# Two transformer blocks on one core: norms cut into a latent and a context half, modulation chunks and rotary tables moved, and a first stage fed chunk by chunk from one queue

## The reference

```python
# first block; for each layer i, for latents and (while needed) context, m = silu(c) @ w_mod[i] + b_mod[i] in 9 parts
def ffn_sublayer(h, shift, scale, gate, w_in, w_out, g, b):
    y = swiglu(h * (1.0 + scale) + shift, w_in, w_out)
    return layer_norm(ALPHA * h + 0.5 * gate * y, g, b)
...
h_lat = ffn_sublayer(h_lat, m_lat[0], m_lat[1], m_lat[2], ...)         # and h_ctx
u_lat, u_ctx = modulate(h_lat, m_lat[3], m_lat[4]), modulate(h_ctx, ...)
y_lat, y_ctx = attention(u_lat, u_ctx, w_qkv, w_o, ...)                # layer 0 neighbourhood, layer 1 windowed
h_lat = layer_norm(ALPHA * h_lat + m_lat[5] * y_lat, g, b)             # and h_ctx in layer 0
h_lat = ffn_sublayer(h_lat, m_lat[6], m_lat[7], m_lat[8], ...)         # and h_ctx in layer 0
```

## Time and profile before

| | |
|---|---|
| median of 3 runs | 2751.87 us (2750.27 to 2756.49) |
| profiled execution | 2755.03 us, span 2753.0 us, mean TensorE clock 0.977 |
| busy: PE / PEld / DVE / ACT / POOL | 2626.1 / 2266.3 / 1631.3 / 1099.2 / 358.3 us |
| moved | 394.24 MB, mean 143 GB/s |

### The profile page before, as it was taken

One profiled execution on the slowest core, in us unless ns is written; L12 is line 12 of the kernel. 1 busy time (PEld: TensorE's weight loads), 2 busy tenths in 40 slices (PEclk: granted clock), 3 DMA queues, 4 the chain that ended last, 5 costly groups with the idle time before them and its releaser, 6 DMA issues.

```text
span 2753.0 us, 41075 instructions
## 1 busy us (share of the span) xinstructions
PE 2626.1 (95%) x16124; PEld 2266.3 (82%) x16124; DVE 1631.3 (59%) x2363; ACT 1099.2 (40%) x1542; POOL 358.3 (13%) x426
## 2 busy tenths in 40 slices
PE   6999998999899998999998989989899999999999
PEld 3888886877688886888887689989899899998989
DVE  4665746566574474575655755565565566565555
ACT  3221223265422223321224653444455445455453
POOL 3000023122300003200013020010001100000210
PEclk8999999999999999999999999999899999999999
DMA  6453524411253352353432035535324454432544
GB/s 241 171 183 124 195 105 141 161 64 46 96 192 132 108 187 80 137 191 138 168 130 101 32 128 186 198 143 191 117 93 153 161 199 168 168 125 77 184 168 146
DMA packets 64252, 394.24 MB, mean 143 GB/s; under 512 B 7440, under 2 KB 8944, under 8 KB 29040
## 3 DMA queue, kind: packets, MB, share of 16 engines
q1 hardware_dynamic: 41072, 308.78, 31.6%
q0 software_dynamic: 21344, 77.41, 8.1%
q10 hardware_dynamic: 1696, 6.08, 0.6%
HBM read 391.19 MB, written 1.05 MB: 142 GB/s over the span
## 4 chain that ended last, share of the span: by engine, by line
PE 84%; DVE 7%; ACT 4%; issue 2%; DMA 1%; POOL 1%; ACTq 0%; POOLq 0%; DVEq 0%
PE banks L412 24%; PE banks L414 24%; PE banks L413 24%; DVE wlo L377 3%; ACT whi L369 3%; PE banks L437 1%; PE banks L1055 1%; PE banks L439 1%; PE banks L438 1%; PE banks L1079 1%; PE banks L1066 1%; DMA shift_start<-in_w_mod 1%; PE banks L427 1%; PE banks L428 1%; PE banks L429 1%
## 5 line engine op out<-in xcount | busy, mean ns | idle before, releaser
L377 DVE TENSOR_TENSOR wlo<-raw,whi 128x2048 fp32r<-128x2048 f32 (+1 forms) x272 | 668.1, 2456 | 449.8 <-ACT whi L369 449.7
L369 ACT CAST whi<-raw 128x2048 fp32r<-128x2048 f32 (+1 forms) x272 | 548.6, 2017 | 278.1 <-PE banks L414 238.6
L412 PE MATMUL banks<-uhi,whi 128*128 128x512 f32 (+1 forms) x1648 | 601.6, 365 | 2.7 <-DVE wlo L377 2.7
L414 PE MATMUL banks<-uhi,wlo 128*128 128x512 f32 (+1 forms) x1648 | 599.8, 364 | 0.0
L413 PE MATMUL banks<-ulo,whi 128*128 128x512 f32 (+1 forms) x1648 | 599.8, 364 | 0.0
L412 PE MATMUL banks<-u2hi,whi 128*128 128x256 f32 x1312 | 375.8, 286 | 4.0 <-DVE wlo L377 3.9
L413 PE MATMUL banks<-u2lo,whi 128*128 128x256 f32 x1312 | 371.9, 283 | 0.0
L414 PE MATMUL banks<-u2hi,wlo 128*128 128x256 f32 x1312 | 371.9, 283 | 0.0
L412 PEld LDWEIGHTS banks<-uhi,whi 128*128 128x128 f32 x1648 | 309.5, 188 | 59.6 <-DVE wlo L377 3.3
L413 PEld LDWEIGHTS banks<-ulo,whi 128*128 128x128 f32 x1648 | 309.5, 188 | 55.3
L414 PEld LDWEIGHTS banks<-uhi,wlo 128*128 128x128 f32 x1648 | 309.4, 188 | 55.1
(11 more groups left out here) (382 smaller groups left out, 3904.5 us busy)
## 6 DMA issues: line engine op xcount, KB each, us to landing
raw<-in_ffn_in SPq DMA_DIRECT2D x132, 1024.0 KB, 4.8
raw<-in_ffn_out SPq DMA_DIRECT2D x48, 1408.0 KB, 6.3
mod_slot<-in_w_mod POOLq DMA_DIRECT2D x128, 512.0 KB, 3.5
raw<-in_w_merge SPq DMA_DIRECT2D x32, 1024.0 KB, 4.7
raw<-in_w_in SPq DMA_DIRECT2D x26, 1024.0 KB, 4.8
raw<-in_na_qkv SPq DMA_DIRECT2D x12, 1024.0 KB, 4.8
raw<-in_w_out SPq DMA_DIRECT2D x8, 1024.0 KB, 4.7
raw<-in_wa_qkv SPq DMA_DIRECT2D x6, 1024.0 KB, 4.8
```

The lines of the kernel that those rows point to most:

```text
L369: act.copy(whi[u % 2][:, 0:unit_size[u]], raw[u % 2][:, 0:unit_size[u]]).then_inc(hi_done, 1)
L377: dve.tensor_tensor(wlo[u % 2][:, 0:n], raw[u % 2][:, 0:n], whi[u % 2][:, 0:n].bitcast(F32), ALU.subtract).then_inc(lo_done, 1)
L412: pe.matmul(out, w_hi, x_hi[:, k, 0:T], start=(n == 0), stop=False)
L414: mm = pe.matmul(out, w_lo, x_hi[:, k, 0:T], start=False, stop=(n == len(chunks) - 1))
```

## The change

The four norms are cut into a latent part 0 and a context part 1 (`PARTS`). The last two out units run their latent halves first, then their context halves; means, variance, centring, scaling, `uhi`, `full_u` and `ulo` are made for 256 tokens at a time. POOL now makes `full_u` for both parts. The weights of the next phase's first unit are split in two pieces inside the norm. The next phase starts with its first unit on latents, then its second on latents, then the first and the second on context; for L1.q only the first unit is special, and the context norm is spread over the q units. Modulation chunks are dealt out anew: three per unit in L0.ffn0.out0, none in the first two units of L0.q. The rotary tables are made during M0.ffn0.out0, in other buffers. At the start, SP issues every load in the order of use, with `h` in four pieces; the scale part is laid out so that one chunk gives 128 features, PE makes one column of scales per chunk, and units 0 and 1 take chunk after chunk, unit 1 four chunks behind. The window tables are loaded before the norm of s=4 instead of behind it.

The helpers not shown do on one part what the functions before did on all tokens: `add_part_dve` adds a product to `h`, `part_var_dve`, `part_centre_dve`, `part_scale_dve`, `part_low_dve` are the variance, the subtraction of the mean, the multiplication by `rstd` and `ulo`; `part_square_act`, `part_rstd_act`, `part_hi_act` square, make `rstd` and `uhi`; `part_sums_pool` and `part_full_pool` add up and make `full_u`; `part_means_pe` is four 256-column float32 matmuls; `part_unit` is one half unit on one part; `split_hi_piece` and `split_lo_piece` split half of a unit's weights. Line numbers of the rows are those of the kernel before.

```diff
+    def part_product(pe, u, half, k, x_hi, x_lo, part, start, stop):
+        a, b = PARTS[part]
+        out = banks[:, bank(u, half), a:b]
+        w_hi, w_lo = cols(whi, u, k, half * P, half * P + P), cols(wlo, u, k, half * P, half * P + P)
+        pe.matmul(out, w_hi, x_hi[:, k, a:b], start=start, stop=False)
+        pe.matmul(out, w_hi, x_lo[:, k, a:b], start=False, stop=False)
+        return pe.matmul(out, w_lo, x_hi[:, k, a:b], start=False, stop=stop)
...
+    def out_in_parts_pe(pe, ph, chunks, x_hi, x_lo, s):
+        u2, u3 = ph.u0 + 2, ph.u0 + 3
+        for u in (u2, u3):
+            start_unit(pe, u)
+            for half in range(2):
+                part_unit(pe, u, half, chunks, x_hi, x_lo, 0).then_inc(latent_product, 1)
+        for cc in range(4, KC):
+            pe.wait_ge(*DVE_.at("h part", s, cc, 0))
+            part_unit(pe, u2 + (cc - 4) // 2, cc % 2, chunks, x_hi, x_lo, 1).then_inc(product, 1)
+            if cc == 4:
+                part_means_pe(pe, s, 0)
...
+    def first_latents_pe(pe, u, s):
+        pe.wait_ge(*DVE_.at("first half lo", u))
+        pe.wait_ge(evicted, u - 1)
+        for k in range(KC):
+            if k == KC // 2:
+                pe.wait_ge(lo_done, u + 1)
+            pe.wait_ge(*DVE_.at("u", s, k, 0))
+            for half in range(2):
+                mm = part_product(pe, u, half, k, uhi, ulo, 0, k == 0, k == KC - 1)
+                if s == 4 and k == KC - 1:
+                    mm.then_inc(product, 1)
+            if k == 3:
+                part_means_pe(pe, s, 1)
+    def first_two_units_pe(pe, ph, s):
+        u0, u1 = ph.u0, ph.u0 + 1
+        first_latents_pe(pe, u0, s)
+        start_unit(pe, u1)
+        for half in range(2):
+            part_unit(pe, u1, half, KC, uhi, ulo, 0)
+        for k in range(KC):
+            pe.wait_ge(*DVE_.at("u", s, k, 1))
+            for half in range(2):
+                mm = part_product(pe, u0, half, k, uhi, ulo, 1, k == 0, k == KC - 1)
+                if k == KC - 1:
+                    mm.then_inc(product, 1)
+        for half in range(2):
+            part_unit(pe, u1, half, KC, uhi, ulo, 1).then_inc(product, 1)
...
-    MOD_FIRST = {"L0.ffn0.in0": 16, "L0.ffn0.out0": 32, "L0.ffn0.in1": 40, "L0.q": 56, "L0.k": 64, "L0.ffn1.in0": 72,
+    MOD_FIRST = {"L0.ffn0.in0": 16, "L0.ffn0.out0": 32, "L0.ffn0.in1": 44, "L0.q": 60, "L0.k": 64, "L0.ffn1.in0": 72,
                  "L0.ffn1.in1": 88, "L1.ffn0.in0": 104, "L1.ffn0.out0": 120, "L1.ffn0.in1": 128}
+    MODS_PER_UNIT = {"L0.ffn0.out0": 3, "L0.k": 2, "L1.ffn0.out0": 2}
 
...
+    def start_loads(sp):
+        def chunk(n):
+            i = n % START_SLOTS
+            if n >= START_SLOTS:
+                sp.wait_ge(*PE_.at("scale column", n - START_SLOTS))
+            sp.dma_start(scale_start[:, i], A["w_mod_scale"][n]).then_inc(scale_landed[i], 16)
+            if n >= START_SLOTS:
+                sp.wait_ge(mod_done, 2 * (n - START_SLOTS + 1))
+            sp.dma_start(shift_start[:, i], A["w_mod"][n]).then_inc(shift_landed[i], 16)
+        def residual(i):
+            sp.dma_start(h[:, 2 * i:2 * i + 2], A["x"][:, 2 * i:2 * i + 2]).then_inc(x_loaded[i], 16)
+        sp.dma_start(crow[:], A["crow"]).then_inc(crow_loaded, 16)
+        sp.dma_start(v1[:], A["vec1"]).then_inc(v1_loaded, 16)
+        chunk(0)
+        load(sp, phases["L0.ffn0.in0"], 0, 0, None)
+        residual(0)
+        chunk(1)
+        chunk(2)
+        residual(1)
+        chunk(3)
+        load(sp, phases["L0.ffn0.in0"], 1, 1, None)
+        chunk(4)
+        residual(2)
+        chunk(5)
+        residual(3)
+        chunk(6)
+        chunk(7)
...
+    def scale_column_pe(pe, n):
+        pe.wait_ge(scale_landed[n % START_SLOTS], 16 * (n // START_SLOTS + 1))
+        if n >= 4:
+            pe.wait_ge(*DVE_.at("start vectors", n - 4))
+        for k in range(KC):
+            mm = pe.matmul(banks[:, 4 + n % 4, 0:2], scale_start[:, n % START_SLOTS, k * P:(k + 1) * P],
+                           c_cols[:, k, :], start=(k == 0), stop=(k == KC - 1))
+        mm.then_inc(*PE_.up(("scale column", n)))
...
+        for n in range(SCALES_AHEAD):
+            scale_column_pe(pe, n)
+        start_unit(pe, 0)
+        for k in range(KC + SECOND_BEHIND):
+            if k + SCALES_AHEAD < KC:
+                scale_column_pe(pe, k + SCALES_AHEAD)
+            if k < KC:
+                pe.wait_ge(*DVE_.at("u", 0, k))
+                chunk(0, k)
+            if k == SECOND_BEHIND:
+                start_unit(pe, 1)
+            if k >= SECOND_BEHIND:
+                chunk(1, k - SECOND_BEHIND)
...
+    def start_vectors_dve(dve, n):
+        at = VEC1["b_mod"][0] + n
+        dve.wait_ge(mod_done, 2 * (n + 1))
+        dve.tensor_scalar(vS0[:, 0, n, :], mods[:, 0, n, :], v1[:, at:at + 1], None, ALU.add).then_inc(*DVE_.up())
+        dve.wait_ge(*PE_.at("scale column", n))
+        dve.tensor_scalar(vS1[:, 0, n, :], banks[:, 4 + n % 4, 0:2], v1[:, at + KC:at + KC + 1], 1.0, ALU.add, ALU.add)\
+            .then_inc(*DVE_.up(("start vectors", n)))
+    def start_dve(dve):
         dve.wait_ge(*ACT_.at("c silu"))
         for n in range(KC):
             mod_products(dve, n, None, shift_start[:, n % START_SLOTS],
                          (shift_landed[n % START_SLOTS], 16 * (n // START_SLOTS + 1)))
-            if n == KC - 2:
+            if n == 0:
+                dve.wait_ge(v1_loaded, 16)
+            start_vectors_dve(dve, n)
+            if n == 0:
                 split_lo(dve, 0)
+                low_dve(dve, 0, T2, 0, uhi, ulo)
+            if n >= 2:
+                low_dve(dve, 0, T2, n - 1, uhi, ulo)
+            if n == 4:
+                split_lo(dve, 1, early=True)
+        low_dve(dve, 0, T2, KC - 1, uhi, ulo)
...
+    def norm_in_parts_dve(dve, s, gated_by, ready):
+        u0 = out_of(s).u0
+        split_lo(dve, u0 + 3)
+        for cc in range(4, KC):
+            add_part_dve(dve, s, cc, 0, gated_by, ready)
+        add_part_dve(dve, s, 4, 1, gated_by, ready)
+        part_var_dve(dve, s, 0)
+        for cc in range(4):
+            part_centre_dve(dve, s, cc, 0)
+        if s == 2:
+            add_part_dve(dve, s, 5, 1, gated_by, ready)
+        else:
+            for cc in range(4, KC):
+                part_centre_dve(dve, s, cc, 0)
+        dve.wait_ge(*ACT_.at("rstd", s, 0))
+        for cc in range(3):
+            part_scale_dve(dve, s, cc, 0)
+        part_low_dve(dve, s, 0, 0)
+        if s != 2:
+            add_part_dve(dve, s, 5, 1, gated_by, ready)
+        part_low_dve(dve, s, 1, 0)
+        split_lo_piece(dve, u0 + 4, 0)
+        for cc in range(3, KC):
+            if s == 2 and cc >= 4:
+                part_centre_dve(dve, s, cc, 0)
+            part_scale_dve(dve, s, cc, 0)
+            part_low_dve(dve, s, cc - 1, 0)
+            if cc == 3:
+                split_lo_piece(dve, u0 + 4, 1)
+                add_part_dve(dve, s, 6, 1, gated_by, ready)
+            if cc == LAST_ADD_AFTER:
+                add_part_dve(dve, s, 7, 1, gated_by, ready)
+        part_low_dve(dve, s, KC - 1, 0)
+        split_lo(dve, u0 + 5, early=True)
+        if s < 4:
+            context_norm_dve(dve, s, range(KC))
+    def context_norm_dve(dve, s, ccs):
+        if ccs[0] == 0:
+            part_var_dve(dve, s, 1)
+            for cc in range(4):
+                part_centre_dve(dve, s, cc, 1)
+            dve.wait_ge(*ACT_.at("rstd", s, 1))
+        for cc in ccs:
+            part_scale_dve(dve, s, cc, 1)
+            if cc < 4:
+                part_centre_dve(dve, s, cc + 4, 1)
+            if cc > ccs[0]:
+                part_low_dve(dve, s, cc - 1, 1)
+        part_low_dve(dve, s, ccs[-1], 1)
...
+    def norm_in_parts_act(act, s):
+        u0 = out_of(s).u0
...
+        for cc in (4, 5, 6):
+            part_square_act(act, s, cc, 0)
+        act.preload_act_table_set("natural_log_exp_and_others")
+        part_square_act(act, s, 7, 0)
+        part_square_act(act, s, 4, 1)
+        part_rstd_act(act, s, 0)
+        for cc in range(2):
+            part_hi_act(act, s, cc, 0)
+        split_hi_piece(act, u0 + 4, 0)
+        part_square_act(act, s, 5, 1)
+        part_hi_act(act, s, 2, 0)
+        split_hi_piece(act, u0 + 4, 1)
+        for cc in range(3, KC):
+            part_hi_act(act, s, cc, 0)
+            if cc == 3:
+                part_square_act(act, s, 6, 1)
+            if cc == LAST_ADD_AFTER:
+                part_square_act(act, s, 7, 1)
+        split_hi(act, u0 + 5, early=True)
+        if s < 4:
+            context_norm_act(act, s, range(KC))
...
+    def norm_in_parts_pool(pool, s):
+        for cc in range(4):
+            part_sums_pool(pool, s, cc, None)
+        for cc in (4, 5, 6):
+            part_sums_pool(pool, s, cc, 0)
+        part_sums_pool(pool, s, 4, 1)
+        for cc in range(KC):
+            part_full_pool(pool, s, cc, 0)
+            if cc == 1:
+                part_sums_pool(pool, s, 5, 1)
+            if cc == 3:
```

(82 more changed lines are left out.)

364 lines of the change are left out of this document (231 added, 133 removed).

## The result

The changed kernel took 2710.59 us (median of four, 2707.16 to 2715.45) beside 2754.18 us for the kernel before on the same chip: ratio 0.9844, 95% interval 0.9823 to 0.9866. The prediction was 2702.5 us with a range of 2687 to 2719. The time is 8.1 us above it. Of these, 2.3 come from the kernel before, whose median is 2754.18 us here and was 2751.87 when the prediction was written: 49.4 us of gain were forecast and 43.6 measured. The terms that fell short are two, the norms and the start. The profiled execution took 2708.93 us, 46.1 less than that of before.

The account below looks back on a forecast made before the run. TensorE, busy 95% of the span, was taken as the bound, leaving only idle and low-clock time to gain. Norms 29.6, start 14.8, modulation 1.4 and tables 3.6 summed to 49.4 us: 2705.6 profiled, 2702.5 median, range 2687 to 2719.

Parts of the forecast that it names:

- slower by the clock: Rival: short waits hold TensorE at 1.2 GHz behind norms and at the start, 50 us slower than now; chance 0.03.
- does nothing: Rival: the chain moves to weights, splits late by a whole norm each time, 2752 us; chance 0.02.
- Hardly a stall: Rival: norms 41, start 18.4, modulation 2.8, tables 4.2, 66 us gained in all, 2686 us; chance 0.1.
- The norms, 29.6 predicted: Four norms hidden under half products: 7.7 each at s=1 and s=3, 5.3 at s=2, 8.9 at s=4; bounds 19, 43.5.
- I take between the ends, near the average row: 1.8 us lost: Norms: stalls from GpSimd's full_u, between none at half a microsecond each and about 4.5 us per norm at 1.25.
- 24.1 to 26.9: Behind an FFN's norm: when u1's split weights are ready, in us after the last out product's latent half; wanted at 24.4.
- s=2, 5.3 predicted: Norm behind L0.wo: cover only 12.9 us; 9.8 less 4.5 for late u1 and u3 weights and GpSimd.
- Rival 1: GpSimd and VectorE shut each other out in every norm; norms give 19, all 39 us, 2713 us; chance 0.2.
- The start, 14.8 predicted: Start through unit 1: its end moves from 71.84 to 57 us, 14.8 gained; bounds 11.8 and 18.4.
- I take 57, nearer the first: Start: unit 1's end, between 53.4 if TensorE kept up and 60 at the upper end of the scale columns' cost.
- Modulation, 1.4 predicted: L0.q's 2.66 us wait goes (2.8 with restart), 1.4 lost at L0.ffn0.out0's end; net 1.4, bounds 0 and 2.8.
- Tables, 3.6 predicted: The 4.20 us wait before M0.z's third unit goes, last squares delayed 0.6; 3.6 gained, bounds 2 and 4.2.

Follow-up runs that it names:

- norms_old: The changed kernel with all four norms back in the old order, new start, modulation chunks and tables kept: 2734.49 us, ratio 0.9929 to the kernel before.
- no_full: The changed kernel without GpSimd's full_u in the norms; VectorE forms ulo from h, shift left out: 2703.39 us, ratio 0.9819 to the kernel before.
- full_unused: The changed kernel with ulo formed from h without the shift, GpSimd still making every full_u, unread by the subtraction: 2705.47 us, ratio 0.9832 to before.
- one_scale: The changed kernel with one of the eight matmuls of each scale column at the start, output not the reference's: 2707.64 us, ratio 0.983 to before.
- best_ahead3: Three start scale columns ahead, not two, against the changed kernel with halved second-unit weights, four full_u buffers, moved third chunk, earlier L0.wo cast: 2709.18 us.

## Why the prediction was near, and where it was off

**That it is faster, with little loss at the low clock:** right. The half products cost what the whole ones did (0.117 us apart at 422 us in after), the granted clock was 0.986 over the span (0.977 before) and 1.00 over the norms s=1 and s=3; behind L0.wo it fell to 0.87 for 13 us, and from 1450 to 1475 us, in L1.q, to 0.96. The rivals "slower by the clock" and "does nothing" are out. "Hardly a stall" (2686) is out too.

**The norms, 29.6 predicted:** 7.1 + 1.1 + 5.7 + 7.6 = 21.5 us measured (by stages, with norms_old to separate s=1 from the modulation). The term that was mis-sized is "I take between the ends, near the average row: 1.8 us lost". Against the ceilings, lost were 9.8 - 7.1 = 2.7 at s=1, 8.7 at s=2, 4.1 at s=3 and 14.0 - 7.6 = 6.4 at s=4. Two things were under-sized. The second unit's weights were put at "24.1 to 26.9" and taken near the middle: they were late by 1.40 us behind s=1, s=3 and s=4 and by 1.09 behind s=2. And GpSimd's full_u, 0.83 us on average and often in pairs, held up VectorE for 13.4 us in all. The two overlap. Taking the wait for full_u away returned 6.3 us and splitting the second units' weights in halves 3.2, of the 8.1 by which the norms fell short (29.6 against 21.5); about half of the 8.1 is the norm s=2.

**s=2, 5.3 predicted, 0.5 to 1.1 measured.** The prediction listed u3's weights 0.7 late (1.40 measured), u1's 2.5 late (1.09), GpSimd 1.0. It had no term for the fourth chunk: 2.53 us. VectorE had no break from 684.00 us to the end of that chunk's `ulo` at 688.1: between the third chunk's `ulo` and this one its queue held a half split (1.42 us), an addition, a centring and a scaling (0.72), and the `ulo` itself took 0.94 us instead of 0.42. TensorE stood idle from 685.6. With the parts order this wait nowhere fell below 1.61 us (no_full), and no run tried another order of these instructions.

**Rival 1 (GpSimd and VectorE shut each other out, 2713):** the time is nearer to it than to the forecast (2.4 us against 8.1; by gains, 43.6 lies 4.6 from its 39 and 5.8 from 49.4), and the norms' sum nearer to its 19. Its mechanism is half right. By the Trainium skill (SBUF — State Buffer, section "Who interferes with whom") the two exclude each other while VectorE uses the shared pair of ports. The trace agrees in that full_u took 0.67 us at its shortest, 0.83 on average and 0.93 when VectorE never waited for it, and a half split 1.59 us instead of 1.33. But full_unused, with all that contention left in, gets 6.3 us back: what was lost there is the dependence on the slower engine. How much of its slowness is contention stays open.

**The start, 14.8 predicted, 12.35 measured:** the step that failed is "I take 57, nearer the first", the first bound being that VectorE limits the start and TensorE keeps up with it; the mis-sized term is the scale columns, put at "1.9 to 3.7 us a chunk". They took 3.4 us each at the low clock, near the upper end. TensorE was never idle from 14.19 us to the end of unit 1, while VectorE waited 1.49 and 2.33 us for two of the columns: TensorE was the bound, and unit 1 ended at 59.5 (57 forecast, the upper end was 60):

```profile
21.04 0.77 PE L643 MATMUL banks<-uhi,whi 128*128 128x512 f32 x1
...
23.75 3.41 PE L633 MATMUL banks<-c_cols,scale_start 128*128 128x2 f32 x16
...
39.12 1.84 PE L633 MATMUL banks<-c_cols,scale_start 128*128 128x2 f32 x16
```

The term is also not one number. Ten executions with the same start had out0 at 157.6 to 157.8 (three), 160.1 to 160.7 (four) or 163.0 to 163.2 (three): gains of 15.0, 12.3 and 9.5 us. An execution of the first kind would have given the 14.8 forecast, by luck.

**Modulation, 1.4 predicted:** 3.8 gained in L0.q and L0.k less 1.5 at the end of out0, 2.3. The loss was sized and placed right; L0.q and L0.k together gave 3.8 where 2.8 was counted, as the low clock behind the 2.66 us wait cost more than the restart that was counted.

**Tables, 3.6 predicted:** TensorE's row in front of M0.z's third unit has no wait any more, where 4.20 us stood:

```profile
1901.35 0.28 PE L534 MATMUL banks<-u2hi,wlo 128*128 128x256 f32 x1
...
1909.65 0.28 PE L542 MATMUL banks<-whi,u2hi 128*128 128x256 f32 x1
```

The lead over before grew from 35.15 us (1936.50 - 1901.35) to 39.59 (1949.24 - 1909.65) there: 4.4, and some of it is clock; ahead of it the lead had dipped from 35.2 to 34.0. No run took the tables back alone, so this term is read from one pair of traces and not shown by an experiment.

**The sum.** 12.35 + 21.5 + 2.3 + 4.4 = 40.5 us by terms; 43.6 by medians; 46.1 in the two profiled executions. The 5.6 us between the terms and these executions arise in the second block, behind M0.z's third unit, where the lead grew from 39.59 to 45.80 us (2747.07 - 2701.27 at TensorE's last row) in instructions that the change leaves as they were. From M0.z's first matmul to TensorE's last row the changed kernels took between 804.5 (after) and 812.9 us (one_scale), so that after's profiled execution is the luckiest of them there. That the forecast came within 5.8 us of the gain is in part luck too: the norms and the start fell 10.6 short, modulation and tables gave 1.7 more, and 3.1 us by medians belong to no term.

## What to carry to other kernels

When whole products are cut so that a norm's work hides under the rest, count every engine's queue up to the first late chunk, and put the unit's weights and the slowest helper's result in that count: the losses here were waits of 1 to 2.5 us on those two, not on the norm. Test a suspected contention by leaving the work in and taking only the dependence away; here that returned 6.3 us, more than leaving out the work itself (5.1). And where terms are smaller than the scatter of whole times, compare stages between landmarks: those of the new order repeated within 0.2 us, one of the old order only within 0.6.

## What the hardware showed that I had not expected

- At the start TensorE's 512-column matmuls stood 0.43 us apart from 21 us on, which is the pace of 1.2 GHz, though the windows' column of granted clock reads 1.00 there (a window over 14 to 44 us of norms_old):

```profile
14.00:44.00 30.00, 29.84 (x121) 27.52 (x122) 24.18 (x43) 10.54 (x18) 11.19 (x5) 1.00 0.96 387
```

- The first 512-column matmuls at twice that pace stood at 31.7 to 32.0, at 37.7 to 38.4 or at 43.8 to 44.1 us, in kernels whose starts are the same. TensorE had been busy without a break since 14 us, some two thirds of the time in the scale columns' matmuls. One doubling earlier or later is worth 2.5 to 3 us. In best_ahead3 and one_scale, with other starts, it came near 39 us.
- A float32 matmul of two columns isn't cheap: a scale column's 16 rows take 3.4 us at the low clock and 1.84 at the high one, 0.21 and 0.115 us each. At the high clock that is what a 256-column row costs in this kernel (0.117). That it is the weights that cost this is a guess; no run varied them.
- A GpSimd addition over 512 columns beside VectorE's 3.01 us split took 3.34 us behind L0.wo, and the split was itself 0.7 us longer: the pair of the earlier trace rows repeats.
